# Two pieces of weights held at the end of each sum, and the second half of x in layer norm on VectorE: a two-block transformer kernel

## The reference, cut to what matters

```python
# first block, i = 0, 1
h = modulate(rms_norm(x, g0), shift, scale);  x = x + 0.5 * gate * swiglu(h)      # 1024 -> 2816 -> 1024
h = modulate(rms_norm(x, g1), shift, scale);  x = x + gate * mixer(h) @ w_out     # fox (i=0), dilated (i=1)
h = modulate(rms_norm(x, g2), shift, scale);  x = x + 0.5 * gate * swiglu(h)
# second block, i = 0, 1
merged = sigmoid(x @ ga) * (na(x) @ wa) + sigmoid(x @ gb) * (retention(x) @ wb)
x = layer_norm(ALPHA * x + merged @ w_out, ln1)
ple = sigmoid(x @ w_ple_gate) * (p @ w_ple_proj)
x = layer_norm(ALPHA * x + conv_glu(x) + ple, ln2)
```

## Time and profile before

| what | value |
|---|---|
| time, median of 3 runs | 2297.67 us (2296.34 to 2298.53) |
| profiled execution: its time | 2295.14 us |
| its span | 2293.8 us |
| PE busy | 2192.3 us, 96% |
| DVE, ACT, POOL busy | 1368.5, 1096.6, 111.1 us |
| mean granted clock of PE | 0.984 |

### The profile page before, as it was taken

The page is one execution under the profiler, slowest core; times in us unless marked ns, Lnnn a source line. Parts: engine busy times, 40 slices in busy tenths (PEclk is TensorE's granted clock), DMA queues, the critical chain, the costliest instruction groups (busy, mean ns, idle before and its releaser), DMA issues.

```text
span 2293.8 us, 33513 instructions
## 1 busy us (share of the span) xinstructions
PE 2192.3 (96%) x14432; PEld 1896.6 (83%) x14432; DVE 1368.5 (60%) x1764; ACT 1096.6 (48%) x1242; POOL 111.1 (5%) x98
## 2 busy tenths in 40 slices
PE   7999998999999999899899999999999999999998
PEld 5997665898799877687699887897998877988996
DVE  4443666644544476666555455567786554578884
ACT  4443565443444354645544345644554356445552
POOL 1100010000000000000000011001000210002000
PEclk9999999999999999999999999999999999999999
DMA  9866672676575756446275565534655554436551
GB/s 356 297 231 245 225 263 75 229 260 243 186 256 189 272 203 229 157 165 214 66 235 184 183 225 174 165 123 142 222 183 195 179 192 139 165 129 211 181 184 49
DMA packets 274819, 448.64 MB, mean 196 GB/s; under 512 B 10816, under 2 KB 146304, under 8 KB 274416
## 3 DMA queue, kind: packets, MB, share of 16 engines
q1 hardware_dynamic: 270016, 429.07, 55.4%
q0 software_dynamic: 4368, 16.31, 2.1%
q10 hardware_dynamic: 288, 1.11, 0.1%
HBM read 445.40 MB, written 1.06 MB: 195 GB/s over the span
## 4 chain that ended last, share of the span: by engine, by line
PE 44%; DVE 3%; ACT 2%; POOL 1%; issue 1%; DMA 0%; POOLq 0%; ACTq 0%
PE ps L1434 43%; DVE wlo L1859 2%; ACT whi L1655 0%; PE ps L1588 0%; ACT L1655 0%; POOL sg L2238 0%; PE ps L1538 0%; POOL x L2197 0%; POOL x L2200 0%; DVE nbuf L1943 0%; DVE x L1899 0%; DMA sg<-in_na_rpb 0%; DVE xs L1923 0%; ACT rtm L1655 0%; PE ps L1621 0%
## 5 line engine op out<-in xcount | busy, mean ns | idle before, releaser
L1859 DVE TENSOR_TENSOR wlo<-raw,whi 128x2048 fp32r<-128x2048 f32 x339 | 785.9, 2325 | 549.7 <-ACT whi L1655 549.3
L1655 ACT ACTIVATE whi<-raw 128x2048 fp32r<-128x2048 f32 x339 | 641.0, 1895 | 425.0 <-PE ps L1434 375.7
L1434 PE MATMUL ps<-xhi,whi 128*128 128x256 f32 x2632 | 648.0, 286 | 7.9 <-DVE wlo L1859 4.1
L1434 PE MATMUL ps<-xhi,wlo 128*128 128x256 f32 x2632 | 641.6, 284 | 0.0
L1434 PEld LDWEIGHTS ps<-xhi,whi 128*128 128x128 f32 x2632 | 506.3, 192 | 23.5 <-issue 14.9
L1434 PEld LDWEIGHTS ps<-xhi,wlo 128*128 128x128 f32 x2632 | 506.5, 192 | 1.2 <-issue 0.7
L1434 PE MATMUL ps<-xlo,whi 128*128 128x256 f32 x2632 | 344.3, 283 | 0.1
L1434 PEld LDWEIGHTS ps<-xlo,whi 128*128 128x128 f32 x2632 | 327.6, 192 | 0.5 <-DVE xlo L1949 0.3
L1434 PE MATMUL ps<-whi,xhi 128*128 128x512 f32 x736 | 299.5, 407 | 16.1 <-DVE wlo L1859 12.5
L1434 PE MATMUL ps<-wlo,xhi 128*128 128x512 f32 x736 | 291.8, 396 | 0.0
L1434 PE MATMUL ps<-whi,hhi 128*128 128x512 f32 x528 | 209.5, 397 | 1.9 <-DVE rows L1883 1.0
(11 more groups left out here) (218 smaller groups left out, 1835.5 us busy)
## 6 DMA issues: line engine op xcount, KB each, us to landing
raw<-in_mod_w SPq DMA_DIRECT2D x72, 1024.0 KB, 9.1
raw<-in_w_in SPq DMA_DIRECT2D x52, 1024.0 KB, 5.1
raw<-in_ffn_w_gate SPq DMA_DIRECT2D x88, 512.0 KB, 6.1
raw<-in_ffn_w_up SPq DMA_DIRECT2D x88, 512.0 KB, 7.4
raw<-in_ffn_w_down SPq DMA_DIRECT2D x44, 1024.0 KB, 6.9
raw<-in_w_up SPq DMA_DIRECT2D x88, 512.0 KB, 4.8
raw<-in_dil_w_in SPq DMA_DIRECT2D x36, 1024.0 KB, 6.0
raw<-in_w_down SPq DMA_DIRECT2D x22, 1024.0 KB, 5.0
```

The source lines that it names most:

```text
L1434: return nc.tensor.matmul(o, lhs, rhs, start=start, stop=stop, skip_group_check=True)
L1655: return nc.scalar.activation(o, i, func, **kw)
L1859: V.tensor_tensor(wlo[:, s["c"], 0:s["n"]], raw[:, s["slot"], 0:s["n"]], whi[:, s["c"], 0:s["n"]].bitcast(F32), ALU.subtract).then_inc(sem ...
```

## The change

The last two pieces of each sum are taken together (`last_two`), and each quarter is run over both; `Tail.step` then adds root and scale of a token half as soon as its second square or moment is added. For the rms norm the first square plus 1e-6 is formed by DVE (`small_term`), and ACT's square root adds the second one to it. In `norm` the mod unit stands ahead of the barrier, and its gate_spread behind the first unit of the stage; that unit takes (D2, D3). Further mod units start behind unit 1, not 0. In the second block the splitting of p and `pleproj` of u = 0 stand ahead of the barrier of layer norm, `pleproj` of u = 1 ahead of `plegate` of u = 1. x = xs * g + b is done by DVE in two halves: the first behind the chunks, the second behind the first unit. In the diff "..." marks lines left out; the DVE and ACT programs change to match, and `branch` to `wout` keep their work.

```diff
@@ -178,6 +179,9 @@
     def next_pair(self):
+        if self.first_pair:
+            pair, self.first_pair = self.first_pair, None
+            return pair
         self.pair ^= 1
...
@@ -243,6 +238,12 @@
         return b0, b1, tok
+    def last_two(self):
+        self.ensure(2)
+        self.ensure(late=True)
+        return self.pieces[self.use], self.pieces[self.use + 1]
...
@@ -307,7 +326,6 @@
             if t:
-                self.run_turns(True)
                 toks = [self.ev("pe", "x_turned") for _ in range(NC)]
...
@@ -345,15 +363,18 @@
-    def norm(self, i, s, tail, between=None):
-        if between:
-            between()
+    def norm(self, i, s, tail):
         toks = self.x_turn("xs", tail.scaled)
-        self.pair = 0
+        self.begin_units()
         self.convert_low()
...
         self.ensure()
+    def begin_units(self):
+        self.pair = 0
+        self.first_pair = (D2, D3) if self.turn_banks[0] == G0 else None
...
@@ -395,64 +416,55 @@
             bank_free = [self.free[b] for b in (D0, D1, D2, D3)]
-        end = q == FB // 2 - 1
...
+        if q == FB // 2 - 2:
+            return
+        if q < FB // 2 - 2:
+            pc = self.take()
+            tok = self.down_step(q, pc, bank_free, ((0, 0), (0, 1), (1, 0), (1, 1)))
             self.used(pc, tok)
...
             return
-        self.ensure(late=True)
+        pcs = self.last_two()
         for t in range(2):
             for h in range(2):
-                tok = self.ev("pe", "piece")
...
+                toks = [self.down_step(q - 1 + n, pc, [], ((t, h),)) for n, pc in enumerate(pcs)]
+                tail.step(t, h, toks[1])
+        for n in range(2):
+            self.used(pcs[n], toks[n])
+    def down_step(self, q, pc, bank_free, parts):
+        tok = self.ev("pe", "piece")
+        self.add("down", q=q, c=pc["c"], w_lo=pc["w_lo"], bank_free=bank_free, need=[self.h_ready[2 * q], self.h_ready[2 * q + 1]],
+                 parts=parts)
+        return tok
+    def out_units(self, src, need, begin, base=D0, beside=False):
         for u in range(2):
-            b0, b1 = G0 + u, G2 + u
+            b0, b1 = base + u, base + 2 + u
             bank_free = [self.free[b0], self.free[b1]]
             pc = self.take()
-            for kk in range(4):
-                tok = self.token_step(pc, need, src, b0, b1, 0, NC, (kk,), bank_free)
-                if kk == 3:
+            for ks in [(kk,) for kk in range(4)] if beside else [range(4)]:
+                tok = self.token_step(pc, need, src, b0, b1, 0, NC, ks, bank_free)
+                if ks[-1] == 3:
                     self.used(pc, tok)
-                self.run_beside()
+                if beside:
+                    self.run_beside()
+            self.run_turns()
         while self.beside:
...
         self.run_turns()
-        pc = self.take()
...
+        pcs = self.last_two()
+        tail = begin()
         for t in range(2):
-            tail.step(t, 0, tok)
...
+            toks = []
+            for u in range(2):
+                toks.append(self.token_step(pcs[u], need, src, base + u, base + 2 + u, 4, NC, range(4), [], (t,)))
+                tail.step(t, u, toks[u])
+        for u in range(2):
+            self.used(pcs[u], toks[u])
+        if src == "x":
+            self.x_read = toks[1]
         return tail
...
@@ -652,32 +657,26 @@
             done = mul
-        tok = pl.ev("dve", "resid")
-        pl.add("update", how=self.kind, t=t, h=h, bank=bank, done=done, x=pl.x_ready[2 * t + h])
-        pl.x_ready[2 * t + h] = tok
+        tok = pl.x_ready[2 * t + h] = self.update(t, h, bank, done)
         if self.kind != "gate":
             pl.free[bank] = tok
-        if self.norm == "rms":
...
+        self.stats = pl.statistics(t, h, self.norm, self.stats if h else [])
+        if h:
+            self.scaled[t] = self.end(t, tok)
+    def update(self, t, h, bank, done):
+        tok = self.plan.ev("dve", "resid")
+        self.plan.add("update", how=self.kind, t=t, h=h, bank=bank, done=done, x=self.plan.x_ready[2 * t + h])
+        return tok
+    def end(self, t, tok):
         pl = self.plan
-        for t in range(2):
...
+        if self.norm == "raw":
+            return tok
+        recip = pl.root(t, self.stats, self.norm)
+        if self.norm == "out":
+            return pl.ln_out(t, recip)
+        return pl.scale(t, self.norm, recip)
...
@@ -799,24 +797,27 @@
         toks = self.x_turn("xs", tail.scaled)
-        self.pair = 0
+        self.begin_units()
         self.convert_low()
         self.x_chunks(range(NC), toks, "ln", lambda m: dict(i=i, j=j))
-        tok = [self.ev("pool", "ln_x") for _ in range(2)][-1]
...
         self.ensure()
+        self.ln_x(0)
+    def ln_x(self, h):
+        tok = [self.ev("dve", "ln_x") for _ in range(2)][-1]
+        self.add("ln_x", h=h, rows_in=[(f"row_in{g}", self.rows_in[g]) for g in range(2)], own=tok)
+        self.x_ready[h] = self.x_ready[2 + h] = tok
...
         self.x_ready[2 * t] = self.x_ready[2 * t + 1] = toks[-1]
+        return toks[-1]
...
         toks = self.x_turn("x", tail.scaled)
-        self.pair = 0
+        self.begin_units()
         self.convert_low()
...
@@ -847,8 +848,11 @@
         b0, b1, tok = self.feature("x", self.need_x) if u < 2 else self.token(self.need_x)
+        self.kept = u, b0, b1, tok
+    def na_kept(self, u, b0, b1, tok):
         t = self.ev("act", "na_kept")
-        self.add("na_keep", u=u, b0=b0, b1=b1, piece=tok, xs_read=self.x_ready[3])
+        self.add("na_keep", u=u, b0=b0, b1=b1, piece=tok, xs_read=self.x_ready[1:])
         self.free[b0] = self.free[b1] = t
...
@@ -950,21 +954,23 @@
         self.p_split = [hi, lo]
-        self.ple_free = None
     def plegate(self, u):
-        b0, b1, tok = self.token(self.need_x)
+        b0, b1, tok = self.token(self.need_x, banks=(D2, D3) if u == 0 else (D0, D1))
         self.ple = self.ev("act", "ple_sig")
-        self.add("plegate", b0=b0, piece=tok, ple_free=self.ple_free)
+        self.add("plegate", u=u, b0=b0, piece=tok)
         self.free[b0] = self.free[b1] = self.ple
...
     def pleproj(self, u):
-        b0, b1, tok = self.token(lambda kc: self.p_split, "p", 2)
+        self.p_done = self.token(lambda kc: self.p_split, "p", 2, banks=(G2, G3) if u == 0 else (G0, G1))
+    def ple_out(self, u):
+        b0, b1, tok = self.p_done
         t = self.ev("dve", "ple_mul")
         t2 = self.ev("dve", "ple_mul")
-        self.add("pleproj", u=u, b0=b0, piece=tok, gate=self.ple, mul=t, x=[self.x_ready[u], self.x_ready[2 + u]])
+        self.add("ple_out", u=u, b0=b0, piece=tok, gate=self.ple, mul=t, x=[self.x_ready[u], self.x_ready[2 + u]])
         self.free[b0] = self.free[b1] = t
-        self.ple_free = self.e_free[0] = self.e_free[1] = t2
+        self.e_free[0] = self.e_free[1] = t2
         self.x_ready[u] = self.x_ready[2 + u] = t2
...
@@ -1003,7 +1009,7 @@
             for n, u in enumerate(fl):
-                at[min(15, (n * 16) // len(fl))].append(u)
+                at[1 + (n * 15) // len(fl)].append(u)
             for q in range(11):
...
@@ -1065,12 +1067,12 @@
                 step("branch", i=i, u=u, b=1)
-            for u in range(2):
-                step("wout", i=i, u=u)
+            step("wout", i=i)
+            step("pleproj", i=i, u=0)
             step("ln", i=i, j=0)
-            for u in range(2):
-                step("plegate", i=i, u=u)
-                step("pleproj", i=i, u=u)
+            step("plegate", i=i, u=0)
+            step("pleproj", i=i, u=1)
+            step("plegate", i=i, u=1)
             for q in range(11):
...
@@ -1152,15 +1151,15 @@
                     self.rows_load("gate_rows", self.x_ready[3], n=n + 1)
+                md = s["m"]
+                self.mod_unit(*md, (D3 if self.turn_banks[0] == D0 else G3) - md[1] % 2, 1)
                 if s["s"] != 1:
...
                     self.fox_begin()
-                md = s["m"]
-                bank = D3 if self.turn_banks[0] == D0 else G3
-                self.norm(i, s["s"], tail, (lambda: self.mod_unit(*md, bank - md[1] % 2, 1)) if md else None)
+                self.norm(i, s["s"], tail)
                 if s["s"] == 1:
...
@@ -1211,19 +1214,21 @@
             elif k == "wout":
-                if u == 1:
-                    tail = Tail(self, "alpha", "mean")
-                self.out_unit(u, "m", lambda kc: self.m_split[kc], tail)
+                self.split_p()
+                tail = self.out_units("m", lambda kc: self.m_split[kc], lambda: Tail(self, "alpha", "mean"))
             elif k == "ln":
...
                     self.layer_norm(i, 0, tail)
-                    self.split_p()
                 elif i == 0:
...
                 self.plegate(u)
+                self.ple_out(u)
+                if u == 0:
+                    self.ln_x(1)
+                    self.rows_load("ln_rows", self.x_ready[1], i=i, j=1)
             elif k == "pleproj":
...
@@ -1922,6 +1928,15 @@
```

(65 more changed lines are left out.)

125 lines of the change are left out of this document (32 added, 93 removed).

## The result

The kernel after takes **2318.18 us** (median; 2316.64 to 2319.13), the kernel before, run beside it, 2297.02 us (2296.34 to 2298.53): a ratio of 1.0091, 95% interval 1.0073 to 1.0108. So the change costs 21 us. The forecast was slower by 9 us, 2306.6 in a range of 2292 to 2320: the sign held and the time lies in the range, but the change costs over twice what was forecast. The profiled execution took 2318.4 us, of which 2317.1 are its span, against 2295.1 and 2293.8 before.

What follows compares the result with a forecast made beforehand. PE was taken as the bound, busy 2192.3 of 2293.8 us. Terms of 11.4 - 0.8 - 4.6 - 2.2 + 5.1 gave +8.9 us, so 2306.6 for the median, in a range of 2292 to 2320.

Steps and rivals of the forecast that it cites:

- The tail: Behind a sum's last product, scale runs from 3.4 to 4.3 us instead of 4.2 to 5.0, saving 0.8 us.
- The second piece: Next stage's second split comes late behind all eight chunks; wlo ends at E+15.4, PE waits 2.8 to 3.1 us.
- The five ends: Sum ends followed by a mod unit: each longer, by +1.5, +1.4, +2.4, +2.6 and +1.5 us.
- 5.1 for the clock: Half clock behind the new waits in three of five ends, priced from one 2.24 us wait: +5.1 us.
- the end behind down2: Layer norm behind down2: third unit begins at 33.0 us, 33.0 against 37.6 in all, -4.6 us.
- Both layer norms behind wout: Stretch ends at 35.1 us if the clock stays, 36.0 to 36.9 at half rate; taken as 0.0 and -0.8.
- A: Whole kernel: the forecast itself, slower by 5 to 16 us; chance 0.48.
- B: Behind the new waits the clock stays up: +3.8 us, 2301.5; chance 0.20.
- C: At the sum ends the held pieces cost nothing, the second wlo being in time: -15.3 us, 2282; chance 0.18.
- D: Each new wait brings 6.8 us at half clock, 3.4 lost: +20.8 us, 2318; chance 0.10.
- E: In layer norm the p product and DVE's x gain nothing: +4.6 us taken back, 2311; chance 0.04.
- The signs: Among them: behind each sum PE's second wait is for DVE wlo, 2.5 to 3.2 us, at E+12 to 13.

Runs made afterwards that it cites:

- Experiment 2: Kernel after, with the modulation unit behind gate/up unit 10 moved back behind unit 9 in feed-forward 2 and 3: 2306.84 us, ratio 1.0031 to the kernel before.
- experiment 1: Kernel before, with the modulation unit behind gate/up unit 9 moved behind unit 10 in feed-forward 2 and 3: 2315.76 us, ratio 1.0075.
- experiment 10: Kernels before and after, both unchanged, each profiled once more: spans of 2295.0 and 2317.6 us.
- experiment 6: Kernel after with that unit behind 9 and second pieces split early everywhere, ln_x halves moved from DVE to POOL: 2311.9 us, ratio 1.0052 to before.
- experiment 9: Kernel before, with 16 more transposes on TensorE in feed-forward 1, a delay of 1.7 us: 2301.74 us, ratio 1.0008.

## Why the prediction was right in sign and wrong in size

**The step that failed** is one that the prediction did not take. Its tail, norm and layer-norm terms cover every edit but the move of the modulation units, which the section on the change gives in one sentence ("Further mod units start behind unit 1, not 0") and the sum costs at nothing. Experiment 2 puts 11 to 14 us on it in the kernel after, experiment 1 17 us in the kernel before. The row was there to be read: each of these units needs a gate/up unit behind it as cover for its row copy and turn, and behind number 10 there is none. Experiment 2 measures what the sum claimed to be: +7 us against +8.9. That the time lay in the range all the same was luck, since the larger part of the 21 us is a term that the sum lacks.

**The tail** came out as worked out: scale at E+3.1 to 4.0 (forecast 3.4 to 4.3), the kept-back wlo at E+4.2, nbuf at E+6.4 (6.5).

**The second piece** too. Its wlo ends at E+15.3 (15.4). PE's second wait is for DVE wlo, in the timeline of after 2.88 us behind feed-forward 1, 2.56 behind fox mixer and 2.59 behind dilated mixer (2.8 to 3.1); behind feed-forward 2 and 3 it is 1.09 and 1.46, because the clock had fallen already in the waits ahead and stretched the first piece, which the prediction allowed for two of five ends. The bank wait of 0.8 is there.

**The five ends** were booked at 9.4 us plus 5.1 for the clock. The stretches of 24.3, 23.7 (fox mixer), 23.0, 22.9 and 24.6 us are 13.0 over those of the earlier trace rows, so the two terms together are 14.5 against 13.0, with the clock in it. By the granted clocks of these stretches (0.93 in all five; before, 0.84, 0.92 and three times 1.00) about 17 us of them ran at half clock, against 10 before, which makes about 3.4 us of the 13.0, where 5.1 were booked. The price behind the 5.1, a row of one execution, did not come again in a second one (experiment 10). The raw end is 16.7 (16.7), the end behind down2 33.1 (33.0). Both layer norms behind wout take 36.8, as before, so the 0.8 that the second was to win are not there; the terms that the prediction lists for them add up to 34.6, not 35.1, which changes nothing in its sum.

**The gains** stand: -4.9 by the shift of the second wout's sum against the first's (the down2 end, -4.6), -2.4 from there to the span's end (-3.0 with the second wout end). But experiment 6 shows that the price of POOL depends on what it stands beside, so -4.6 is the worth of this move only.

**The rivals.** The measured +21 lies above A's own 5 to 16 us. B and C fall: the clock did not stay up (0.93 in the stretches behind all five) and the held pieces did cost. D named 2318, the number measured, for a wrong reason: it wanted 6.8 us at half clock behind each new wait, where each of the five ends has 3.4, and the missing 12 us came from a place that it did not name. E falls, since the end behind down2 has its gain. A right total is no sign of a right cause.

**The signs** given for right were seen, but for one: behind feed-forward 2 and 3 the second wait is shorter than 2.5 us and begins about 14 us behind the sum, not 12 to 13.

## What to carry to other kernels

When a change moves work, list every step that it moves, and for each one the work that hid it before and the work that hides it now; a formula of places is best written out as the list of places in each stage. A piece that a tail holds must be paid for by the first unit behind it, and the order of splits and chunks there is worth as much as the tail: here, with the modulation unit back in its place, splitting the second piece early turned a loss of 7 us into a gain of 10. Edits that look independent (early root, held pieces) can need each other, so undo them one at a time before you drop any.

## What the runs showed that was not expected

- Longer half-clock stretches need not cost time where PE waits for DVE or ACT afterwards: in two executions of one program (experiment 10) the one with 4.8 us less of PE's busy time took 1.2 us longer. Behind the first wout the half-clock stretch shrank by 3.4 us, the next wait for a wlo grew from 0.33 to 1.39, and the time to the end of down2 stayed the same. A count of such stretches is no price; a 5 us difference in one stage of one profiled execution (experiment 9) is no result either.
- Behind feed-forward 2 and 3 PE waited 1.14 and then 1.6 us, one wait close behind the other, and then ran 3.4 us at 1.2 GHz; ahead of `down`, 6.8 us of it began right behind the wait of 2.50 us in both stages. Both profiles of after show all four. But the length of the waits does not settle it: behind feed-forward 1 the same pair of 1.14 and 1.59 us brought none, and the wait of 2.24 us brought 3.4 us in one profile of before and none in the other. The Trainium skill, TensorE: Matmul & The Clock Gate, "Why this matters for your kernels", allows idle gaps up to about 3 us; these rows do not bear that out.
- A raw piece that is held for PE stops SP's queue for all pieces behind it, here for 13.6 us in before, in after and in experiment 1. What it costs depends on which piece stands next: only in experiment 1 was it the weights that ACT wanted next.
